# Differential attention: the order of scores, mixing and maxima of successive heads

## The reference, cut to what matters

```
s = q @ k.T                      # two maps m = 0, 1 per head, q/k of 64 columns
s = where(key <= query, s, -1e30)
pr = softmax(s)                  # float32
attn = pr[0] - lam * pr[1]
o = attn @ v                     # v of 128 columns
o = rms_norm(o, subln_g) * (1 - lam_init)
```

## Time and profile before

| | us |
|---|---|
| median of 3 runs | 1937.41 |
| lowest, highest | 1930.62, 1937.73 |
| profiled execution, its own time | 1937.56 |
| its span in the trace | 1935.7 |
| TensorE busy in the span | 1827.3 (94%) |
| VectorE busy | 1518.1 (78%) |
| ScalarE busy | 1204.0 (62%) |
| mean granted TensorE clock | 0.975 of full |

### The profile page before, as it was taken

One profiled execution on the slowest core, in us unless ns is written; L12 is line 12 of the kernel. 1 busy time (PEld: TensorE's weight loads), 2 busy tenths in 40 slices (PEclk: granted clock), 3 DMA queues, 4 the chain that ended last, 5 costly groups with the idle time before them and its releaser, 6 DMA issues.

```text
span 1935.7 us, 31866 instructions
## 1 busy us (share of the span) xinstructions
PE 1827.3 (94%) x10685; PEld 1449.0 (75%) x10685; DVE 1518.1 (78%) x2100; ACT 1204.0 (62%) x1624; POOL 54.3 (3%) x90
## 2 busy tenths in 40 slices
PE   6888898999999897999999999999999999999998
PEld 5665567888876655577788888888888888888886
DVE  5874666655578756574899999999999999999997
ACT  4632445555556223452678778777887788778775
POOL 2000000000020000000300000000000000000000
PEclk9999999999999998998999999999999999999999
DMA  8522163565554311443799999999999999999993
GB/s 259 166 91 65 55 212 99 168 192 185 186 179 131 107 46 45 146 148 130 272 369 346 356 364 343 370 353 349 375 337 361 353 352 377 336 364 348 362 365 145
DMA packets 224014, 474.54 MB, mean 245 GB/s; under 512 B 16680, under 2 KB 41400, under 8 KB 223376
## 3 DMA queue, kind: packets, MB, share of 16 engines
q1 hardware_dynamic: 219456, 458.29, 67.2%
q0 software_dynamic: 3472, 13.65, 2.2%
q10 hardware_dynamic: 960, 1.10, 0.2%
HBM read 468.25 MB, written 1.05 MB: 242 GB/s over the span
## 4 chain that ended last, share of the span: by engine, by line
PE 54%; DVE 1%; issue 0%; ACT 0%; DVEq 0%
PE psum L465 16%; PE psum L467 16%; PE psum L466 16%; PE psum L1011 2%; PE psum L1058 1%; PE psum L1022 0%; PE psum L1023 0%; PE psum L489 0%; PE psum L882 0%; PE psum L572 0%; PE psum L870 0%; ACT SH L1459 0%; PE psum L1103 0%; DVE x L2214 0%; DVE y_lo L2154 0%
## 5 line engine op out<-in xcount | busy, mean ns | idle before, releaser
L465 PE MATMUL psum<-w_hi,h_hi 128*128 128x512 f32 (+1 forms) x1648 | 653.0, 396 | 31.5 <-DVE w_lo L419 29.5
L467 PE MATMUL psum<-w_hi,h_lo 128*128 128x512 f32 (+1 forms) x1648 | 643.7, 391 | 0.0
L466 PE MATMUL psum<-w_lo,h_hi 128*128 128x512 f32 (+1 forms) x1648 | 643.6, 391 | 0.0
L465 PEld LDWEIGHTS psum<-w_hi,h_hi 128*128 128x128 f32 x1648 | 312.1, 189 | 106.1 <-DVE w_lo L419 24.8
L467 PEld LDWEIGHTS psum<-w_hi,h_lo 128*128 128x128 f32 x1648 | 312.3, 189 | 66.5
L466 PEld LDWEIGHTS psum<-w_lo,h_hi 128*128 128x128 f32 x1648 | 312.7, 190 | 62.5 <-issue 0.5
L405 ACT ACTIVATE w_hi<-ring,col 128x512 fp32r<-128x512 f32 (+1 forms) x232 | 150.8, 701 | 125.6 <-PE psum L467 112.9
L419 DVE SCALAR_TENSOR_TENSOR w_lo<-ring,col,w_hi 128x512 fp32r<-128x512 f32 (+1 forms) x232 | 163.3, 751 | 81.7 <-ACT w_hi L405 80.2
L435 DVE TENSOR_TENSOR w_lo<-ring,w_hi 128x1024 fp32r<-128x1024 f32 x144 | 172.2, 1220 | 7.6 <-ACT w_hi L431 3.1
L431 ACT ACTIVATE w_hi<-ring 128x1024 fp32r<-128x1024 f32 x144 | 151.9, 1060 | 41.0 <-PE psum L467 41.0
L435 DVE TENSOR_TENSOR w_lo<-dproj,w_hi 128x1024 fp32r<-128x1024 f32 x120 | 145.8, 1222 | 17.3 <-ACT w_hi L431 14.0
(11 more groups left out here) (316 smaller groups left out, 2329.7 us busy)
## 6 DMA issues: line engine op xcount, KB each, us to landing
ring<-in_expert_w_gu SPq DMA_DIRECT2D x128, 512.0 KB, 5.5
SH<-in_expert_w_gu SPq DMA_DIRECT2D x120, 512.0 KB, 5.9
proj<-in_expert_w_gu SPq DMA_DIRECT2D x104, 512.0 KB, 6.2
dproj<-in_expert_w_gu SPq DMA_DIRECT2D x72, 512.0 KB, 5.9
dproj<-in_expert_w_down SPq DMA_DIRECT2D x72, 512.0 KB, 5.2
ring<-in_expert_w_down SPq DMA_DIRECT2D x64, 512.0 KB, 5.1
ring<-in_in_proj SPq DMA_DIRECT2D x48, 512.0 KB, 5.2
ring<-in_dense_w_gu SPq DMA_DIRECT2D x88, 256.0 KB, 3.1
```

The lines of the kernel that those rows point to most:

```text
L465: pe.matmul(o, h[0], w[0], start=start, stop=False, skip_group_check=True)
L466: pe.matmul(o, h[0], w[1], start=False, stop=False, skip_group_check=True)
L467: return pe.matmul(o, h[1], w[0], start=False, stop=stop, skip_group_check=True)
```

## The change: what it does

TensorE: the scores of heads 0 and 1 come first, then two memory blocks, as before. From there the scores of head h+2 are issued right behind the transposition of head h (before: the scores of head h+1 at the head of pass h, behind the values of head h-1), and a memory block stands behind the values of each of the first three heads. The memory blocks are as many as before.

ScalarE: the copy of the transposed mix of head h now stands ahead of the exponentials of head h+1, and the values' result behind them. With the copy, `diff_proj` of head 0's transposition (the take-out of the second key chunk) also stands ahead of the exponentials of head 1.

VectorE: the mixing of head h stands ahead of the maxima of head h+1 (before: behind them). Pieces of `finish()`: before two behind every pass; now one between maxima and mixing of heads 1 to 3, and behind the mixing of head h min(h, 2).

```diff
                 diff_scores(0)
-                for h in range(4):
-                    if h < 3:
-                        diff_scores(h + 1)
-                    some(kv, (2, 1, 1, 1)[h])
+                diff_scores(1)
+                some(kv, 2)
+                for h in range(DH):
                     pe.wait_ge(attn_ready, 4 * l + h + 1)
                     bank = open_work(("atT", l, h))
...
                     B.filled(last, ("atT", l, h))
+                    if h < DH - 2:
+                        diff_scores(h + 2)
                     some(kv, 1)
                     B.wait_evacuated(pe, ("atT", l, h))
                     bank = open_work(("pv", l, h))
...
                     B.filled(pe.matmul(bank[:, 128:256], aT[:, h % 2, 256:384], vv[1], start=False, stop=True), ("pv", l, h))
+                    if h < DH - 1:
+                        some(kv, 1)
...
-                for h in range(DH):
+                def diff_exp(h):
                     for m in range(2):
                         ahead(("ds", l, h, m))
                         act.wait_ge(smx, 8 * l + 2 * h + m + 1)
...
-                    if h:
-                        diff_out(h - 1)
-                diff_out(DH - 1)
...
+                diff_exp(0)
+                for h in range(DH):
+                    diff_proj(("atT", l, h))
+                    copy(W1[:, 512 * (h % 2):512 * (h % 2) + 384], ("atT", l, h), lambda b: b[:, 0:384])
+                    if h < DH - 1:
+                        diff_exp(h + 1)
+                    diff_out(h)
...
-                for h in range(DH + 1):
-                    if h < DH:
-                        row_max(h)
+                for h in range(DH):
+                    row_max(h)
                     if h:
-                        attend(h - 1)
-                    for _ in range(2):
+                        next(rest_of_y, None)
+                    attend(h)
+                    for _ in range(min(h, 2)):
                         next(rest_of_y, None)
```

More of the change, by code:

```diff
@@ L1395, in _ @@
                                     copy(qk[:, which, :, qt * P:(qt + 1) * P], ("qkT", l, which, qt))
-                def diff_out(h):
-                    diff_proj(("atT", l, h))
-                    copy(W1[:, 512 * (h % 2):512 * (h % 2) + 384], ("atT", l, h), lambda b: b[:, 0:384])
-                    name = ("pv", l, h)
-                    diff_proj(name)
-                    ahead(name)
-                    bank = B.wait_filled(act, name)
-                    for t in range(TT):
-                        j = 4 * h + t
-                        src = bank[:, t * DV:(t + 1) * DV]
-                        act.activation(qs[:, 256 * (h % 2) + t * DV:256 * (h % 2) + (t + 1) * DV], src, ACT.Square, scale=rcp[:, j:j + 1], accum_out=osq[:, 4 * t + h:4 * t + h + 1])
-                        ins = act.activation(hNv[:, t, RW + h * DV:RW + (h + 1) * DV], src, ACT.Copy, scale=rcp[:, j:j + 1])
-                    B.release(ins, name)
-                for h in range(DH):
+                def diff_exp(h):
                     for m in range(2):
@@ L1421, in _, with diff_out @@
                         ins.then_inc(pexp, 1)
-                    if h:
-                        diff_out(h - 1)
-                diff_out(DH - 1)
+                def diff_out(h):
+                    name = ("pv", l, h)
+                    diff_proj(name)
+                    ahead(name)
+                    bank = B.wait_filled(act, name)
+                    for t in range(TT):
+                        j = 4 * h + t
+                        src = bank[:, t * DV:(t + 1) * DV]
+                        act.activation(qs[:, 256 * (h % 2) + t * DV:256 * (h % 2) + (t + 1) * DV], src, ACT.Square, scale=rcp[:, j:j + 1], accum_out=osq[:, 4 * t + h:4 * t + h + 1])
+                        ins = act.activation(hNv[:, t, RW + h * DV:RW + (h + 1) * DV], src, ACT.Copy, scale=rcp[:, j:j + 1])
+                    B.release(ins, name)
+                diff_exp(0)
[5 more added lines that the diff above has]
+                    diff_out(h)
                 diff_proj(("hT", l, 1, 0, 0))
```

## The result

The changed kernel took 1926.03 us (median of 4 runs, 1925.71 to 1927.97), the kernel before on the same chip 1937.57 (4 runs). The ratio is 0.995 with a 95% interval of 0.9932 to 0.9969. Forecast was 1927.1. The profiled execution took 1925.88.

What follows compares the result with a forecast made beforehand. TensorE was taken to bound the kernel (busy 1827.3 of 1935.7 us), so the gain is its idle or slow time. 1937.5 less 10.4 (6.2 in layer 0, 4.2 in layer 1) gave 1927.1 us; 8-in-10 range 1921.5 to 1933.

Steps and rivals of the forecast that it cites:

- The waits for the mix vanish: Ahead of the transpositions: TensorE's gaps of 3.52 (layer 0), 1.92 (layer 1) and 0.66 us at heads 1 and 2 go.
- The cover of 3.4 us: Transposition of head 1, layer 0: mix ready at 222.5, TensorE there at 225.94, so ScalarE's part could be 3.4 longer.
- The new wait in layer 0: Scores of head 3 wait 1.3 us for VectorE's take-out of head 2's banks, behind the inverse square root.
- No wait in layer 1: Scores of head 3: second bank out at 776.85, TensorE there at 777.04, so no wait, 0.2 us of cover.
- TensorE's path: From the two memory blocks to head 3's transposition: 33.6 us in layer 0 and 32.3 in layer 1.
- The sum of 32.28: TensorE's work on that stretch without waits: 8 memory blocks, three transpositions, two pairs of scores, three of values, in us.
- The tail: From head 3's transposition to the result's second half: 10.1 us, with the 1.2 us gap staying.
- Rival 3: Behind the heads: output projection's blocks land too late for an earlier TensorE, time stays 1937.5 us; chance 0.07.
- The sum: Both layers' heads: 6.2 us less in layer 0 and 4.2 in layer 1, together 10.4, of which 1.7 is clock.
- The clock (rival 1): Memory blocks or layer 1's recurrence: the slow stretch stays or returns elsewhere, giving back 1.7 us; time 1928.8; chance 0.25.
- The 1.70 us: Layer 0, memory block behind the 3.52 us gap: 5.13 us instead of 3.43 at 0.67 clock, counted as gain.

Runs made afterwards that it cites:

- the held exponentials: The changed kernel with three unused 128x1024 copies on ScalarE ahead of the exponentials of heads 1, 2 and 3; 1933.19 us, ratio 0.9988.
- the tail was filled: The changed kernel with one memory block moved behind the first half's transposition, norm pieces and ScalarE's copy also moved; 1925.97 us, ratio 0.9945.
- the last group: The changed kernel with a memory block moved to the tail, then three versions with GpSimd's vector loads later; 1925.97, 1930.09, 1923.91, 1921.34 us.
- calm: Against the tail-filling kernel with later vector loads and an earlier VectorE split: those loads moved to the middle of the feed-forward part; 1921.34 us, ratio 0.9912.

## Why the prediction held, step by step

- **The waits for the mix vanish.** Right. The brackets of 3.52, 1.92 and those of 0.66 have no successor. The mix of head 1 was through at 222.26, predicted 222.5 (222.3 with the start 0.21 earlier). TensorE was at the transposition of head 1 at 225.97, predicted 225.73 with the same shift. The cover of 3.4 us was tested with the held exponentials, where no transposition waited: three copies took 3.25 us there, the mix of head 1 was through some 0.4 before TensorE came to it.
- **The new wait in layer 0.** Right in place, releaser and size: 1.08 us in the bracket, 1.15 as the difference of stretches when the inverse square root was moved away; 1.3 was predicted. It depends on ScalarE's and TensorE's new order too: undoing either removes it.
- **No wait in layer 1.** Right. The cover was 0.2 in the sum and 0.55 in the trace.
- **TensorE's path.** Predicted 33.6 and 32.3, measured 33.82 and 32.67. The sum of 32.28 was 0.4 short, with nothing waiting. The rows show where: the two first blocks took 217.06 - 210.09 = 6.97 instead of 6.86, and a transposition with scores right behind 217.48 - 217.06 = 0.42 instead of 0.37. The rest is with the blocks behind scores, which start more slowly (their row is 3.70 long, other blocks' 3.60).
- **The tail.** 10.10 and 10.07 us with a gap of 1.20 and 1.16; 10.1 was predicted. Rival 3 did not occur. It was not far: when the tail was filled, one gap of this kind (1.75) appeared at once, beside two of VectorE's order.
- **The sum.** 10.4 us forecast (6.2 and 4.2 by layer), 9.9 in the stretches that the change touches (6.07 and 3.85 with the tails), 11.5 between the medians. That the median came within 1.1 us of the forecast is luck in part: the same kernel's median was 1923.70 in another series. The 1.8 us beyond the stretches are not the change's: in fourteen traces the start alone took 206.9 to 213.8 us, and the stretch between the layers 498.6 to 509.0.
- **The clock (rival 1).** The 1.70 us did vanish in the profiled executions of after. That the order did it is only half shown. The clock was low behind gaps of 3.52 (twice), 4.37 and once of 1.92 us, and full behind another of 1.92 and behind 2.0 to 2.8. Each time it was low cost 1.6 to 1.7 us from start to start. Where no gap in the heads and the tail was over 1.4 us, the clock was full through both. So "no long gap, no slow stretch" fits all traces, but a gap near 2 us is a matter of the execution or of something that no run here separates. By the Trainium skill ("TensorE: Matmul & The Clock Gate", the clock gate) the same kernel may show differing slow counts from run to run. The two traces with the 1.92 us gap fit that, but they are of two kernels, so they don't test it.

What I had not seen is which engine's order matters. I had worked out the whole change and found it right; the parts show that VectorE's order alone is worth 6.08 us in layer 0, as much as the whole change (6.04), and 2.75 of 3.86 in layer 1. TensorE's order alone is worth 1.86 and 0.06 in the profiled executions (in layer 1 the slow clock took away the rest), and on top of the other two it costs 1.1 in layer 0.

## What to carry to other kernels

If a short step on one engine releases the bounding engine, put it ahead of the next long piece of its own queue; work that nobody waits for goes where the bounding engine asks for nothing. Asking for the next banks early turns every lateness of the engine that empties them into a stop, so after such a change look for the next wait at the opening of banks. And where runs scatter by more than the gain, compare stretches inside the traces: one repeated to 0.02 us here, while medians of the same kernel differed by 2.3.

## What the runs showed of the hardware that I had not expected

- The scatter of runs of one program (1930.26 to 1943.12 us for the kernel before within one series) shows in the start and in the stretch between the layers, where TensorE's granted clock is below full (0.94 and 0.91), and hardly in the long last stretch (1125.3 to 1129.1 in fourteen traces, at 0.99).
- A memory block at 128x512 took 3.43 us from start to start at full clock. Behind a gap with the clock at 0.67 to 0.68 it took 5.1 to 5.2, three times; behind the fourth (0.72) the transposition and scores came first and took part of the slow time, and the block took 4.13.
- Two transfers of 1280 and 1024 KB on GpSimd's queue beside SyncE's weight blocks went with a wait of ScalarE of 4.6 to 7.0 us for a block in all four kernels of the last group. TensorE lost 0.25 us by it in calm, and 1.4 to 2.3 in the others.
